# A two-block network on one core: both ends of the program split and reordered, the logarithms turned four columns at a time

## The reference, cut to what matters

```python
# the first thing: x is normed by rows, then multiplied by w_in
xn = rmsnorm(x, norm1_g[l])
...
# the three groups are mixed by a softmax over their log denominators
alpha = jax.nn.softmax(jnp.stack(lses, axis=0), axis=0)
o_a = jnp.sum(alpha[..., None] * jnp.stack(outs, axis=0), axis=0)
...
# the last thing: x + y @ w_out, and a norm by rows
return rmsnorm_2(h, final_norm)
```

## Time and profile before

| what | us |
|---|---|
| median of 3 runs | 2045.33 |
| lowest and highest | 2044.92 to 2047.1 |
| the profiled execution's own time | 2047.23 |
| its span, from first to last instruction | 2045.4 |
| TensorE busy in it | 1997.9 |
| VectorE, ScalarE busy | 1051.0, 768.9 |

### The profile page before, as it was taken

The page is one execution under the profiler, slowest core; times in us unless marked ns, Lnnn a source line. Parts: engine busy times, 40 slices in busy tenths (PEclk is TensorE's granted clock), DMA queues, the critical chain, the costliest instruction groups (busy, mean ns, idle before and its releaser), DMA issues.

```text
span 2045.4 us, 22770 instructions
## 1 busy us (share of the span) xinstructions
PE 1997.9 (98%) x9515; PEld 1652.3 (81%) x9515; DVE 1051.0 (51%) x1411; ACT 768.9 (38%) x1229; POOL 80.1 (4%) x132
## 2 busy tenths in 40 slices
PE   7999999999999999999999999999999999999897
PEld 6899987888888888888888888888888788866666
DVE  4444447444445337543244455555554565856675
ACT  4555553342423323432233222222222314376763
POOL 0000000000000000000000000000000000033431
PEclk9999999999999999999999999999999999999899
DMA  5222222223232232333333332333233345210002
GB/s 205 64 82 63 82 83 67 90 86 103 67 103 79 86 103 83 103 96 94 100 102 86 101 103 83 103 103 98 89 102 101 101 124 153 78 41 22 32 21 62
DMA packets 186422, 181.24 MB, mean 89 GB/s; under 512 B 4816, under 2 KB 162896, under 8 KB 186320
## 3 DMA queue, kind: packets, MB, share of 16 engines
q1 hardware_dynamic: 182832, 172.41, 27.4%
q10 hardware_dynamic: 3488, 7.38, 1.3%
HBM read 173.49 MB, written 4.19 MB: 87 GB/s over the span
## 4 chain that ended last, share of the span: by engine, by line
PE 83%; DVE 8%; ACT 6%; issue 2%; DMA 1%; ACTq 0%; SPq 0%; DVEq 0%
PE bank L906 75%; DVE tl L2158 2%; ACT tmp L1164 2%; PE bank L1012 1%; DVE rs L2141 1%; ACT raw L1164 1%; ACT wh L1180 1%; PE bank L1001 1%; PE bank L1144 1%; DVE wl L1637 1%; PE bank L1118 1%; DVE oT L2167 1%; PE bank L1040 1%; ACT th L1543 1%; ACT pb L1164 0%
## 5 line engine op out<-in xcount | busy, mean ns | idle before, releaser
L906 PE MATMUL bank<-xh,wh 128*128 128x512 f32 x1352 | 535.2, 396 | 2.1 <-DVE wl L1637 1.5
L906 PE MATMUL bank<-xh,wl 128*128 128x512 f32 x1352 | 527.6, 390 | 0.0
L906 PE MATMUL bank<-xl,wh 128*128 128x512 f32 x1352 | 527.1, 390 | 0.0
L1637 DVE TENSOR_TENSOR wl<-raw,wh 128x2048 fp32r<-128x2048 f32 (+2 forms) x154 | 342.3, 2225 | 267.7 <-ACT wh L1180 267.6
L1180 ACT CAST wh<-raw 128x2048 fp32r<-128x2048 f32 (+2 forms) x154 | 285.2, 1854 | 384.8 <-PE bank L906 372.0
L906 PEld LDWEIGHTS bank<-xh,wh 128*128 128x128 f32 x1352 | 253.8, 188 | 55.8 <-issue 3.3
L906 PEld LDWEIGHTS bank<-xh,wl 128*128 128x128 f32 x1352 | 253.5, 188 | 54.3
L906 PEld LDWEIGHTS bank<-xl,wh 128*128 128x128 f32 x1352 | 253.9, 188 | 51.2 <-issue 0.7
L906 PE MATMUL bank<-wh,xh 128*128 128x512 f32 x512 | 213.8, 418 | 4.2 <-DVE xl L2185 4.0
L906 PE MATMUL bank<-wl,xh 128*128 128x512 f32 x512 | 202.0, 394 | 0.0
L906 PE MATMUL bank<-wh,xl 128*128 128x512 f32 x512 | 201.8, 394 | 0.0
(11 more groups left out here) (271 smaller groups left out, 2594.7 us busy)
## 6 DMA issues: line engine op xcount, KB each, us to landing
raw<-in_w_in SPq DMA_DIRECT2D x50, 1024.0 KB, 5.0
raw<-in_a_w_in SPq DMA_DIRECT2D x32, 1024.0 KB, 5.7
raw<-in_w_up SPq DMA_DIRECT2D x16, 1024.0 KB, 5.4
raw<-in_w_down SPq DMA_DIRECT2D x16, 1024.0 KB, 5.7
raw<-in_w_proj_b SPq DMA_DIRECT2D x8, 1024.0 KB, 5.1
raw<-in_a_w_out SPq DMA_DIRECT2D x8, 1024.0 KB, 5.7
raw<-in_w_out SPq DMA_DIRECT2D x4, 1024.0 KB, 5.0
raw<-in_w_kv SPq DMA_DIRECT2D x4, 1024.0 KB, 5.0
```

Source lines behind the costliest of these rows:

```text
L906: m = e.matmul(o, p, q, start=k == 0 and n == 0, stop=k == K - 1 and n == 2)
L1637: m = e.tensor_tensor(lo, r, hi, ALU.subtract)
```

## The change

Start: SP issues x blocks 0 and 1, then `base`, then x blocks 2 and 3. The first weight block comes in two transfers, the first of its four parts alone (256 KB), then `vec`, then the other three parts (768 KB), and `w_part` waits for the one or the other.

Middle: `mix_turn` is gone with `lseT` and the picks. `mix_pick` transposes four columns of `mx` twelve times, so that the same four rows come out at the same places.

End: the norm of a row block is done in halves. `bo_gain(b)` multiplies half 0 by its gain on VectorE as soon as half 0 of that block is squared, and turns its sum of squares into sum/D + eps. The root takes the sum of half 1, with this as its bias. `bo_end(b)` then multiplies half 0 by the reciprocal on ScalarE and half 1 by reciprocal and gain on VectorE. Each half is written out by a transfer of its own. In the list, `bo_gain` 0 to 2 stand before the last product of c = 0, `bo_gain(3)` behind the first half of the products of c = 1, and `bo_end(b)` behind `("bo", 1, b + 1)`.

Besides, the semaphore `rs_hi` of the retention is counted on `out_a`.

```diff
-    extra += [(at + ATT["log"], ("mix_log",)), (at + ATT["lse"], ("mix_turn",)), (at + ATT["pick"], ("mix_pick",))]
+    extra += [(at + ATT["log"], ("mix_log",)), (at + ATT["pick"], ("mix_pick",))]
...
-    o += flat(fill) + pieces
+    o += flat(fill) + pieces + [("bo_gain", b) for b in range(3)]
     o += flat(steps_of("bo", 0, 3, 1)) + [("w_piece", ("bo", 1, 1), x) for x in range(4)]
-    o += flat(steps_of("bo", 1, 3, 0) + [t for b in range(4) for t in steps_of("bo", 1, b, 1)])
+    o += flat(steps_of("bo", 1, 3, 0)) + [("bo_gain", 3)]
+    for b in range(4):
+        o += flat(steps_of("bo", 1, b, 1)) + ([("bo_end", b - 1)] if b else [])
+    o.append(("bo_end", 3))
...
+    final_gains = [fg[:, x * 512:(x + 1) * 512].rearrange("p (j q) -> p j q", j=4) for x in range(2)]
...
-        def mix_turn():
-            bank = take("aux", ("lse",), ("lseT",))
-            w.wait_ge(*told("lse"))
-            e.transpose(bank[0:48, 0:128], mx, ident).then_inc(*tell("lse_turned"))
-
         def mix_pick():
             for g in range(3):
                 bank = take("aux", ("pick", g), ("mix_w", g))
-                w.wait_ge(*told("lseT"))
-                w.wait_ge(*told("dist"))
+                w.wait_ge(*told("lse"))
                 for b in range(4):
                     o = order(bank[0:4, :], TURN[g])[:, b, :] if g else bank[0:4, b * 128:(b + 1) * 128]
-                    m = e.matmul(o, pick[:, g, b, :], lseT[:, :], start=True, stop=True)
+                    m = e.transpose(o, mx.rearrange("p (g h b) -> p g b h", g=3, h=4)[:, g, b, :], ident)
...
         def w_part(k):
-            w.wait_ge(*told("raw0", 0))
+            w.wait_ge(*told("rest" if k else "first"))
...
-        def mix_turn():
-            w.wait_ge(*told("lse_turned"))
-            e.copy(lseT[:, :], bank_of("aux", ("lse",))[0:48, 0:128]).then_inc(*tell("lseT"))
-
...
             if c:
+                w.wait_ge(*told("ss", key))
                 w.wait_ge(*told("ssum", b))
-                act(ss[:, b, 5:6], ss[:, b, 4:5], ACT.Sqrt, bias=eps[:, 0:1], scale=1.0 / D).then_inc(*tell("sd", "fin", b))
+                act(ss[:, b, 5:6], ss[:, b, 1:2], ACT.Sqrt, bias=ss[:, b, 4:5], scale=1.0 / D).then_inc(*tell("sd", "fin", b))
+
+        def bo_end(b):
+            w.wait_ge(*told("rc", "fin", b))
+            w.wait_ge(*told("ssum", b))
+            act(xo(b, 0), xo(b, 0), ACT.Copy, scale=ss[:, b, 6:7]).then_inc(*tell("out_a", "fin", b))
...
-            if c:
-                w.wait_ge(*told("ss", key))
-                e.tensor_reduce(ss[:, b, 4:5], ss[:, b, 0:2], AX, ALU.add).then_inc(*tell("ssum", b))
-                w.wait_ge(*told("sd", "fin", b))
-                e.reciprocal(ss[:, b, 6:7], ss[:, b, 5:6]).then_inc(*tell("rc", "fin", b))
-                w.wait_ge(*told("rc", "fin", b))
-                w.wait_ge(*told("fg"))
-                stt(xo(b), xo(b), ss[:, b, 6:7], fg[:, :].rearrange("p (j q) -> p j q", j=8), ALU.mult,
-                    ALU.mult).then_inc(*tell("fin", b))
+
+        def bo_gain(b):
+            w.wait_ge(*told("ss", ("bo", 0, b)))
+            w.wait_ge(*told("fg"))
+            e.tensor_scalar(ss[:, b, 4:5], ss[:, b, 0:1], 1.0 / D, EPS, ALU.mult, ALU.add)
+            e.tensor_tensor(xo(b, 0), xo(b, 0), final_gains[0], ALU.mult).then_inc(*tell("ssum", b))
+
+        def bo_end(b):
+            w.wait_ge(*told("sd", "fin", b))
+            e.reciprocal(ss[:, b, 6:7], ss[:, b, 5:6]).then_inc(*tell("rc", "fin", b))
+            w.wait_ge(*told("rc", "fin", b))
+            w.wait_ge(*told("fg"))
+            stt(xo(b, 1), xo(b, 1), ss[:, b, 6:7], final_gains[1], ALU.mult, ALU.mult).then_inc(*tell("fin", b))
...
-        e.dma_start(base[:, :], a["c_base"]).then_inc(*tell("base", by=16))
         for b in range(4):
+            if b == 2:
+                e.dma_start(base[:, :], a["c_base"]).then_inc(*tell("base", by=16))
             e.dma_start(xn[:, b, :], a["x"][0, b * 128:(b + 1) * 128, :]).then_inc(*tell(f"x{b}", by=16))
-        e.dma_start(vec[:, :], a["vecs"]).then_inc(*tell("vec", by=16))
...
+            if n == 0:
+                for x, (k, K) in enumerate(((0, 1), (1, 3))):
+                    e.dma_start(raw[0][:, k * 512:(k + K) * 512].rearrange("p (k c) -> p k c", k=K),
+                                rows_of(m, r0 + k * 128, K, c0, C)).then_inc(*tell("rest" if x else "first", by=16))
+                    if k == 0:
+                        e.dma_start(vec[:, :], a["vecs"]).then_inc(*tell("vec", by=16))
...
         for b in range(4):
-            w.wait_ge(*told("fin", b))
-            e.dma_start(out[0, b * 128:(b + 1) * 128, :].rearrange("p (j q) -> p j q", j=8), xo(b)).then_inc(
-                *tell("out", b, by=16))
-        w.wait_ge(*told("out", 3))
+            for c in range(2):
+                w.wait_ge(*(told("fin", b) if c else told("out_a", "fin", b)))
+                e.dma_start(out[0, b * 128:(b + 1) * 128, c * 512:(c + 1) * 512].rearrange("p (j q) -> p j q", j=4),
+                            xo(b, c)).then_inc(*tell("out", b, c, by=16))
+        w.wait_ge(*told("out", 3, 1))
```

More of the change, by code:

```diff
@@ L671, in program @@
                 dist = sb("dist", [128, 1584], F32, ph)
-                lseT = sb("lseT", [48, 128], F32, ph)
                 with ExitStack() as ph2:
@@ L726, in program @@
     x_mid = nc.dram_tensor("x_mid", (4, 128, D), F32, kind="Internal").ap()
-    pick = dist[0:48, 1024:1072].rearrange("p (g b h) -> p g b h", g=3, b=4)
     alpha = alphas[:, 0:1536].rearrange("p (g t) -> p g t", g=3)
@@ L1150, in end @@
             S_.close(phase, "pe")
-        follow(x_in, x_raw, sum_squares, mm, turn_qk, scores, probs, values, mix_turn, mix_pick, mix, decay, ret, gated_ret,
+        follow(x_in, x_raw, sum_squares, mm, turn_qk, scores, probs, values, mix_pick, mix, decay, ret, gated_ret,
                turn_rs, compress, compressed_k, compressed_v, gates, cmp_scores, cmp_turn,
@@ L1345, in decay_parts @@
                 w.wait_ge(*told("ret", h - 1, 3))
-            e.copy(rsh[kb][:, :], ret_low(kb)[0]).then_inc(*tell("rs_hi", h, kb))
+            e.copy(rsh[kb][:, :], ret_low(kb)[0]).then_inc(*tell("out_a", "decay", h, kb))
         def next_decay(h):
@@ L1587, in end @@
                 e.dma_start(dec[:, :], dec_v[:, 0, :]).then_inc(*tell("dec", 0, by=16))
-        follow(w_, w_part, w_piece, x_norm, x_in, x_raw, square, root, norm, v, rv, q, k_, norm_qk, turn_qk, scores, probs, values, mix_log, mix_turn, mix_pick, rq, rk,
+        follow(w_, w_part, w_piece, x_norm, x_in, x_raw, square, root, norm, v, rv, q, k_, norm_qk, turn_qk, scores, probs, values, mix_log, mix_pick, rq, rk,
                decay_parts, next_decay, rg, ret, gated_ret, ga, pb, split_oa, gb, pa, wo, up, down, z, ao, nsa_consts, fold, vsw, gate,
                hidden, compressed_v, nq_, cmp_scores, cmp_turn, scores_n, turn_n, gather, nz, silu, split_o,
-               final_gain, x_out, bo, end)
+               final_gain, x_out, bo, bo_end, end)
     def vector(e):
@@ L1815, in decay_parts @@
         def decay_parts(h, kb):
-            w.wait_ge(*told("rs_hi", h, kb))
+            w.wait_ge(*told("out_a", "decay", h, kb))
             decayed, low = ret_low(kb)
@@ L2210, in vector @@
                compressed_v, gates, nq_, rope_q, vsw, cmp_scores, cmp_turn, scores_n, rate, turn_n, gather, gate_o,
-               split_o, bo,
-               end)
+               split_o, bo, bo_gain, bo_end, end)
     def pool(e):
@@ L2246, in sync @@
             m = a[matrix]
-            if kind == "pair":
+            if n == 0:
[4 more added lines that the diff above has]
+                        e.dma_start(vec[:, :], a["vecs"]).then_inc(*tell("vec", by=16))
+            elif kind == "pair":
                 for f in range(2):
```

## The result

| | before | after |
|---|---|---|
| median, us (21 runs of each, side by side) | 2045.6 | 2042.88 |
| lowest, us | 2044.48 | 2041.54 |
| ratio after to before, 95% interval | | 0.9984, 0.9978 to 0.9989 |
| span of the profiled execution | 2045.4 | 2042.4 |
| its own time | 2047.23 | 2044.23 |

The change takes off about 3.3 us (0.16%; the interval reaches from 2.2 to 4.5), and 3.0 us of the profiled span. The forecast was 3.4 us off and 2041.9 us; it lies within the bound of 0.2%, though the interval excludes that nothing changed. The sum came out nearly right. Its terms did so only in part: one of them had the wrong sign in this execution, and two effects that it left out partly made up for each other.

A forecast was written before the change was run, and what follows sets the result against it. TensorE, busy 98% of the span, bounds the kernel, so only its idle or lost stretches count. Start 0.15, middle 0.55 and end 2.7 sum to 3.4 us off 2045.33, giving 2041.9 us; 8-in-10 range 2039.9 to 2044.2.

The forecast's parts named there:

- What bounds: Whole kernel: TensorE busy 98% of the span, so only stretches where it idles or loses work count.
- Start, 0.15 us: First loads: x block 0 issued 0.45 us earlier, last x block limits; 0.15 us gained, ends 0.0 and 0.45.
- First weight block, zero: Start: splitting the first weight block gives nothing, since TensorE has 17 transposes to do before using the weights.
- Middle, 0.55 us: Turn of the logarithms: TensorE saves about 1.5 us, mostly returned as waiting at the spread; 0.55 us gained.
- The microsecond's wait for `alpha`: Middle: TensorE would newly wait about a microsecond for alpha before the third spread matmul.
- End, 2.7 us: Last norm in halves: VectorE stops lagging, the last four writes become the bound; 2.7 us gained.
- All other edits move no wait: Rest of the kernel: the renamed semaphore and one aux bank fewer in the rotation move no wait.
- (a): Rival, middle and end: computed waits don't bind; 1.7 instead of 0.55, or 3.9 instead of 2.7; chance 0.2.
- (b): Rival: less gained, start nothing and end 2.2, or extra half clock eats it; 2.0 off, 2043.3 us; chance 0.2.
- (c): Rival, end: half multiplies hold up VectorE, the lag stays, only the middle is left; 2044.7 us; chance 0.04.
- (d): Rival, end: the writes don't overlap, each pays its whole way; 7.0 us slower, 2052.3 us; chance 0.03.
- three conditions named as making it wrong: No TensorE wait at the spread, gaps between the last four writes, or TensorE's last matmul moving over a microsecond.

The follow-up runs named there:

- start_only: Kernel before with only the new load order and the split first weight block; 2046.31 us, ratio to before 0.9999.
- one_block: Kernel after with the first weight block loaded in one transfer instead of two; 2043.43 us, ratio to before 0.9986.
- mix_late: Kernel after with the first mix step six matmul steps later in the written order; 2042.11 us, ratio to before 0.9977.
- best: Kernel after with base behind all x blocks, first mix step later, bo_end directly behind its block, 2048-byte write pieces; 2040.56 us, ratio to before 0.9971.
- end_only: Kernel before with only the last norm in halves; 2042.83 us, ratio to before 0.9984.
- packed: Kernel after with finished halves in contiguous buffers, written in pieces of 2048 bytes instead of 512; 2041.27 us, ratio to before 0.9978.
- mid_only: Kernel before with only the new turn of the logarithms; 2046.14 us, ratio to before 1.0002.
- base_last: Kernel after with base issued behind all four x blocks instead of between blocks 1 and 2; 2041.37 us, ratio to before 0.9976.

## Why the prediction was right or wrong

**What bounds.** TensorE in the stretches where it has nothing to do, and the two ends: right. What was left out is that the stretch between dense start and full clock counts half, and that its end moves by itself.

**Start, 0.15 us: the step failed.** Two things were wrong. The step that took x block 3 for the one that limits failed: it is block 2, which now has `base` in front of it. I counted bytes up to the end of block 3, which are the same in both orders, and never asked for those up to block 2. Signs: the first square at 4.49 (4.6 expected), the fourth at 9.82 (9.1 to 9.2), dense at 12.32 (11.65). And a gain in the dense start was put down as time at full value, though the prediction itself had read the half clock from the pitch of the transposes: `start_only` had 0.48 and kept 0.10. On average over the profiles the order is worth nothing.

**First weight block, zero: right**, by `one_block`, and for the reason given (17 transposes as cover).

**Middle, 0.55 us: right in mechanism, 0.36 in size.** The price of the four-column transpose, taken from 128-column ones, was right: 1.47 us with the last one's drain, 0.103 from start to start, against 1.35. The microsecond's wait for `alpha` came as two, 0.22 and 0.69, and was where it was expected. The term that was too large is how much earlier `alpha` comes: 0.2 in the sum, 0.1 measured, and VectorE still has gaps of about 0.1 between the operations that wait for the picks, though these are long there. That a wait costs it something even then is how I read it; no run tested it. TensorE also begins 0.15 us behind the end of each `alpha` that it waits for, and the product behind the third follows after 0.40 instead of 0.33, where 0.08 was taken in all. That the wait takes the rest is shown by `mix_late`. Up to the spread the account ends well; what the new turn costs near 2023 was not in it.

**End, 2.7 us: right, 2.60.** From the last product's end: first of the last four writes issued after 2.44 (2.38 in the sum), data behind it 0.91 (1.36), 1 MB in 3.81 (3.6), the rest 0.75 (0.5); 7.91 against 7.84. Errors nearly cancel. I read the last write of before wrongly: its data start 1.18 us behind the issue and end 0.75 ahead of the span's end, not 1.36 and 0.5. A 256 KB write starts its data sooner still, and the rate with ramps is 276 GB/s rather than 292. That VectorE would no longer lag, that ScalarE's two halves would stand one behind the other, and that the table load would lie where nobody waits, are all in the rows above.

**"All other edits move no wait": wrong.** This put at nothing what fewer instructions do to the rest of the program. The load of the last row block takes 0.8 to 1.6 us longer than in before in every kernel with the new turn, and TensorE loses 0.45 to 1.20 us near 2023. In after the 0.60 gained near 1709 more than covers it, by chance as far as these runs tell: with the new turn nine of ten profiles gain 0.4 to 0.6 there and `best` loses 0.9, but `end_only`, without it, moves there too, by 0.4 the other way.

**The rivals.** (a), waits that don't bind: they did bind, both. What it promised for the middle was had at the spread by moving one step (`mix_late`), 1.38 us more; the end's better value, 3.9 off, was not reached, and longer pieces brought it to 3.57 (10.50 to 6.93, `packed`). (b): its half-clock part is real, and it goes both ways: by S most of the 1.06 us lost at the start (0.88 from the later full clock, 0.26 from the dense start), and part of the 0.64 gained between 1790 and 2020. (c) did not happen. (d), writes that don't overlap: refuted. Each took 2.4 to 3.5 us to land, but the last four together needed 3.81 us of data. The fixed part is paid once, ahead of a row of transfers in flight.

**The time.** 2041.9 forecast, 2042.88 measured, 1.0 above; before had a median of 2045.6 in the runs beside it, 0.3 above the one on which the forecast stood. The ratio itself, 3.3 us, agrees with the sum of 3.4. None of the three conditions named as making it wrong occurred: TensorE waits at the spread, the last four writes flow without a gap, and the last product is only 0.37 us earlier. The third of these held by luck, since at 290 us TensorE was 1.06 late and got as much back later on, from the weight block near 1709 and between 1790 and 2020, less 0.45 at 2023; the signs of the start are what showed the error.

## What to carry to other kernels

When loads are reordered, count the bytes in front of each block that somebody waits for, not only in front of the last. A saving on the engine that leads becomes a wait unless the first user of the slower chain is moved as well; look for it ahead of time and move it in the same change. Then follow the lead to the last product: a load that comes later than before can take it back 1700 us on, even where the change didn't touch it. At the very end of a kernel the last bytes go out at the rate of their pieces: lay the last results out so that the pieces are long.

## What the runs showed of the hardware

- Writes from on-chip memory to HBM in pieces of 512 bytes run at 274 to 293 GB/s in half-microsecond windows (after), in pieces of 2048 bytes at 381 to 393 (`packed`), with the DMA engines equally busy. Over the last MB it is 276 against 363.
- From issue to first data it is 1.19 us for a write of 512 KB and 0.91 for one of 256 KB; the last data end 0.75 us ahead of the span's end.
- A transpose that reads four columns and writes four rows costs TensorE 0.103 us from start to start, like one of 128 columns.
- An instruction fetch of 16 KB among the packets of a 512 KB load goes with a load of 4.86 to 5.62 us instead of 3.99 to 4.11 (ten profiles against three).
- TensorE's full clock was granted between 14.6 and 17.6 us in thirteen profiles of nearly the same start, which moves what follows by up to 2.0 us (S 12.9 to 14.9). Behind 1790 us half the clock was granted for 6.8 to 17.1 us in all; TensorE's lead over before changed there by -0.3 (`mid_only`, 17.1) to 2.7 us (`base_last`, 6.8). Each is of the size of the whole change.
